# Expert tokens fetched and added back by indirect DMA instead of one-hot matmuls, and expert weights in 4 MB loads over a ring of six units

## The reference, cut to what matters

```python
def expert_choice_moe(xn, w_router, w_gate, w_up, w_down):
    cap = EC_CAPACITY * T // N_EXPERTS            # 2 * 528 // 16 = 66 tokens per expert
    aff = jax.nn.softmax(logits, axis=-1)         # logits = xn @ w_router
    gate, idx = lax.top_k(jnp.swapaxes(aff, 1, 2), cap)
    xe = xn[bidx, idx]                            # 66 rows of 1024 per expert
    hid = jax.nn.silu(xe @ w_gate) * (xe @ w_up)  # w_gate, w_up: 1024 x 2048 per expert
    ye = (hid @ w_down) * gate[..., None]         # w_down: 2048 x 1024 per expert
    return jnp.zeros_like(xn).at[bidx, idx].add(ye)

h = h + expert_choice_moe(rms_norm(h, norm2_g[l]), ...)
return rms_norm(h, final_norm_g)[:, N_META:]
```

## Time and profile before

| | us |
|---|---|
| three timed runs | 2084.88, 2087.76, 2091.49; median 2087.76 |
| profiled execution | 2077.59 |
| its span, first to last instruction | 2075.8 |
| PE busy | 1845.2 (89%) |
| DVE busy | 1356.4 (65%) |
| ACT busy | 1004.0 (48%) |
| POOL busy | 126.2 (6%) |
| queue of SP's and ACT's data (q1), share of 16 engines | 59.5%, 466.12 MB |
| instruction loads (q8) | 187 packets, 3.06 MB |

### The profile page before, as it was taken

One profiled execution on the slowest core, in us unless ns is written; L12 is line 12 of the kernel. 1 busy time (PEld: TensorE's weight loads), 2 busy tenths in 40 slices (PEclk: granted clock), 3 DMA queues, 4 the chain that ended last, 5 costly groups with the idle time before them and its releaser, 6 DMA issues.

```text
span 2075.8 us, 46825 instructions
## 1 busy us (share of the span) xinstructions
PE 1845.2 (89%) x21395; PEld 1346.2 (65%) x21395; DVE 1356.4 (65%) x900; ACT 1004.0 (48%) x627; POOL 126.2 (6%) x101
## 2 busy tenths in 40 slices
PE   4898999889999999946998989898988889899986
PEld 3544863678778888845667666666666667666662
DVE  4422452264343334248899889988988899889994
ACT  4321231142123222134766666676667676667672
POOL 0414043202000000000000000000000000000000
PEclk9798999899999999957999989999999999999997
DMA  9000310123103642005999999999999999999991
GB/s 309 21 21 1 94 34 1 61 62 108 36 21 138 208 151 75 1 26 199 420 380 372 363 378 367 367 363 382 364 357 361 381 374 365 373 380 377 358 362 41
DMA packets 102978, 469.59 MB, mean 226 GB/s; under 512 B 4283, under 2 KB 49659, under 8 KB 86076
## 3 DMA queue, kind: packets, MB, share of 16 engines
q1 hardware_dynamic: 102224, 466.12, 59.5%
q10 hardware_dynamic: 556, 0.32, 0.1%
HBM read 464.32 MB, written 2.10 MB: 225 GB/s over the span
## 4 chain that ended last, share of the span: by engine, by line
PE 64%; DVE 16%; issue 12%; ACT 5%; POOL 2%; DMA 1%; SPq 0%; DVEq 0%; ACTq 0%; POOLq 0%
PE ps_all L1010 22%; DVE wl L941 7%; PE ps_all L1254 6%; PE ps_all L1255 5%; PE ps_all L1256 5%; PE ps_all L1033 5%; PE ps_all L1091 4%; PE ps_all L1242 3%; ACT wh L603 3%; PE ps_all L1240 3%; PE ps_all L1241 3%; PE ps_all L1266 2%; PE ps_all L1222 2%; DVE h L949 2%; DVE tmp L766 1%
## 5 line engine op out<-in xcount | busy, mean ns | idle before, releaser
L941 DVE SCALAR_TENSOR_TENSOR wl<-slot,wh 128x4096 f16<-128x4096 f32 x192 | 847.0, 4419 | 87.4 <-ACT wh L603 87.2
L603 ACT ACTIVATE wh<-slot 128x4096 f16<-128x4096 f32 x192 | 689.3, 3614 | 139.6 <-PE ps_all L1256 90.1
L1240 PE MATMUL ps_all<-xcur,wl 128*128 128x66 f16 x4096 | 402.6, 194 | 46.2 <-DVE wl L941 25.1
L1242 PE MATMUL ps_all<-xcur,wh 128*128 128x66 f16 x4096 | 402.8, 197 | 32.3 <-issue 32.2
L1240 PEld LDWEIGHTS ps_all<-xcur,wl 128*128 128x128 f16 x4096 | 384.7, 100 | 67.8 <-issue 59.4
L1241 PE MATMUL ps_all<-xcur,wh 128*128 128x66 f16 x4096 | 402.4, 194 | 11.3 <-issue 11.3
L1242 PEld LDWEIGHTS ps_all<-xcur,wh 128*128 128x128 f16 x4096 | 383.9, 98 | 37.9 <-issue 37.9
L1241 PEld LDWEIGHTS ps_all<-xcur,wh 128*128 128x128 f16 x4096 | 384.4, 97 | 31.1 <-issue 30.8
L1010 PE MATMUL ps_all<-xnt,wsp 128*128 128x272 f16 (+1 forms) x2688 | 309.6, 278 | 7.0 <-DVE rot L800 5.2
L1010 PEld LDWEIGHTS ps_all<-xnt,wsp 128*128 128x128 f16 x2688 | 265.0, 99 | 52.1 <-issue 8.4
L1254 PE MATMUL ps_all<-wh,hidt 128*66 128x512 f16 x512 | 206.3, 403 | 9.2 <-issue 7.3
(11 more groups left out here) (183 smaller groups left out, 1676.5 us busy)
## 6 DMA issues: line engine op xcount, KB each, us to landing
slot<-in_w_exp_gate SPq DMA_DIRECT2D x64, 2048.0 KB, 9.5
slot<-in_w_exp_up SPq DMA_DIRECT2D x64, 2048.0 KB, 9.8
slot<-in_w_exp_down SPq DMA_DIRECT2D x64, 2048.0 KB, 9.5
raw<-in_w_in SPq DMA_DIRECT2D x32, 1024.0 KB, 5.9
raw<-in_w_ret_out SPq DMA_DIRECT2D x4, 1024.0 KB, 13.6
raw<-in_w_hy_out SPq DMA_DIRECT2D x4, 1024.0 KB, 7.9
raw<-in_w_o SPq DMA_DIRECT2D x4, 1024.0 KB, 5.1
dft_f<-in_c_dft_f SPq DMA_DIRECT2D x1, 2640.0 KB, 20.1
```

Source lines behind the costliest of these rows:

```text
L603: nc.scalar.activation(wh[c % RING][:, :], slot[c % RING][:, :], ACT.Copy, scale=W_S).then_inc(S["w_hi"], 1)
L941: nc.vector.scalar_tensor_tensor(wl[i][:, :], slot[i][:, :], W_S, wh[i][:, :], ALU.mult, ALU.subtract).then_inc(S["w_lo"], 1)
L1240: nc.tensor.matmul(dst, lo, xcur[:, k, 0, :], start=k == 0 and t % TIL == 0, stop=False, skip_group_check=True)
L1242: last = nc.tensor.matmul(dst, hi, xcur[:, k, 1, :], start=False, stop=k == KD - 1, skip_group_check=True)
```

## The change

**Token rows by DMA.** Two DRAM copies are made after the second norm: `h_rows` (the residual) and `xn2_rows` (the normed tokens), both 528 x 1024 float32, stored by POOL. For each expert POOL issues an indirect DMA that fetches 66 rows of `xn2_rows` into `xg` (66 x 1024), named by the column `tok[:, e]` of row numbers, and later one that adds the 66 rows of `ye` to `h_rows` in DRAM. PE turns `xg` with eight float32 transposes in place of the 80 matmuls. `sel`, `st`, `xn2p`, `idxb`, `blki`, `iota`, the scatter and `add_out` go. The gate is applied where ACT takes `ye` out of PSUM. POOL's order is: fetch(0), fetch(1), add(0), fetch(2), add(1), and so on; fetch(e) waits for PE's transposes of expert e - 1, and add(e) for `ye` and for the landing of add(e - 1).

**Weights in 4 MB loads.** A load now brings two units, into one of three slots of 4 MB, so the ring holds six units in place of four. SP waits until both units of the pair three before have their low parts. ACT and DVE still work unit by unit, and `wh`/`wl` remain a ring of four. Three pairs are loaded early (two between the earlier weights, the third after the output projection).

**Ends.** The norm's row `g2b` is loaded before the output projection is done, in place of after it. At the end the four groups of 128 rows are read back from `h_rows` into `hfin`, and the last norm works there.

```diff
+PAIRS = 3
+PAIR_CH = MOE_CH // 2
...
-        def moe_src(e, c):
+        def moe_src(e, j):
+
+            if j < 4:
+
+                m = w_gate if j < 2 else w_up
+                return m[e].rearrange("(p k) n -> p k n", k=KD)[:, 4 * (j % 2):4 * (j % 2) + 4, :]
+
+            return w_down[e].rearrange("(t p) n -> p t n", p=128)[:, 8 * (j - 4):8 * (j - 4) + 8, :]
...
+        def unit(c):
+
+            return pair_slot[c // 2 % PAIRS][:, 4096 * (c % 2):4096 * (c % 2) + 4096]
...
-                if n >= C_A + 1 and n < C_A + 5:
+                if n in (C_A + 1, C_A + 3):
                     if n == C_A + 1:
                         sp.wait_ge(S["yain_split"], KD)
-                    load_first(n - C_A - 1)
+                    load_first((n - C_A - 1) // 2)
...
+            sp.wait_ge(S["tile_done"], AT[("YB", KD - 1)] + 1)
+            sp.dma_start(g2b[:, :], A["norm2_g"][0].partition_broadcast(128)).then_inc(S["g2_row"], 16)
             sp.wait_ge(S["tile_done"], AT[("WO", 3, NT - 1)] + 1)
...
+            load_first(2)
...
             with sp.Fori(1, E) as e:
-                for c in range(MOE_CH):
-                    load(e, c, e * MOE_CH + c - RING + 1)
+                for j in range(PAIR_CH):
+                    load(e, j, e * MOE_CH + 2 * (j - PAIRS + 1))
+            sp.wait_ge(S["rows_landed"], 32 + 16 * E)
+            for k in range(1, NT):
+                sp.dma_start(hfin[:, k - 1, :], h_rows[TS[k][0]:TS[k][0] + 128, :]).then_inc(h_back[k - 1], 16)
...
+            def fetch(e):
+
+                if e:
+                    pool.wait_ge(S["xe_done"], e)
+                pool.indirect_dma_start(xg[:, :], None, xn2_rows[:, :],
+                                        bass.IndirectOffsetOnAxis(ap=tok[:, e:e + 1], axis=0)).then_inc(S["x_in"], 16)
+
+            def add_rows(e):
+
+                pool.wait_ge(S["ye_ready"], e + 1)
+                pool.wait_ge(S["rows_landed"], 32 + 16 * e)
+                pool.indirect_dma_start(h_rows[:, :], bass.IndirectOffsetOnAxis(ap=tok[:, e:e + 1], axis=0),
+                                        ye[:, :], None, compute_op=ALU.add).then_inc(S["rows_landed"], 16)
+
+            for e in range(E):
+                if e + 1 < E:
+                    fetch(e + 1)
+                add_rows(e)
...
             def ye_out(e):
                 act.wait_ge(S["chunk_used"], e * MOE_CH + 12)
+                act.wait_ge(S["rows_landed"], e * 16 + 32)
+                nc.scalar.activation(ye[:, :], ps_all[0:CAP, 3072:4096], ACT.Copy, scale=gate[:, bass.ds(e, 1)]).then_inc(S["ye_ready"], 1)
...
             def gather(e):
 
-                pe.wait_ge(S["sel_ready"], (e + 1) * NT)
+                pe.wait_ge(S["x_in"], 16 * e + 16)
                 for kk in range(KD):
                     c = 512 * (kk // 4) + CAP * (kk % 4)
-                    for k, (_, p) in enumerate(TS):
-                        for q in range(2):
-                            last = nc.tensor.matmul(ps_all[:, c:c + CAP], xn2p[0:p, k, q, kk:kk + KD * 127 + 1:KD], sel[0:p, k, :],
-                                                    start=k == 0 and q == 0, stop=k == NT - 1 and q == 1)
+                    last = nc.tensor.transpose(ps_all[:, c:c + CAP], xg[:, kk:kk + KD * 127 + 1:KD], ident[0:CAP, 0:CAP])
...
-            def scatter(e, k):
...
                 for c in range(MOE_CH):
...
-                    if 2 <= c < 6 and not first:
-                        scatter(e - 1, c - 1)
```

More of the change, by code:

```diff
@@ L137, in job_list @@
     add(("AT",), "work_in", 1)
-    add(("C",), "cols_in", 1)
-    for i in range(2):
-        add(("R", i), "idx_row", i + 1)
+    add(("C",), "cols_in", 2)
     return jobs
@@ L225, in build @@
         ybin = sb("ybin", [128, KD, 2, T], F16, YB)
[L226 to L227 removed]
         xcur = sb("xcur", [128, KD, 2, CAP], F16, XN)
[L229 to L233, removed]
+        hidt = sb("hidt", [128, 2, 16 * CAP], F16, XN + 2112)
+        sg = sb("sg", [128, 16 * CAP], F32, XN + 6336)
+        hid = sb("hid", [128, 16 * CAP], F32, XN + 10560)
+        ye = sb("ye", [CAP, D], F32, XN + 14784)
+        xg = sb("xg", [CAP, D], F32, YA)
+        hfin = sb("hfin", [128, NT - 1, D], F32, YA)
+        gfb = sb("gfb", [128, D], F32, YA + 16384)
         raw = [sb(f"raw{i}", [128, KD, CW], F32, RAW + 8192 * i) for i in range(3)]
         wsp = [sb(f"wsp{i}", [128, 2, KD, CW], F16, SPL + 8192 * i) for i in range(3)]
[L236 to L242, removed]
+        pair_slot = [sb(f"slot{i}", [128, 8192], F32, TOP + 32768 * i) for i in range(PAIRS)]
+        spl_at = [SEARLY, SEARLY + 16384, SLATE, SLATE + 16384]
         wh = [sb(f"wh{i}", [128, 4096], F16, at) for i, at in enumerate(spl_at)]
         wl = [sb(f"wl{i}", [128, 4096], F16, at + 8192) for i, at in enumerate(spl_at)]
[L245 to L247 removed]
+        g2b = sb("g2b", [128, D], F32, SLATE)
+        junk2 = sb("junk2", [128, D], F32, SLATE + 4096)
+        xn2t = sb("xn2t", [128, KD, T], F32, SLATE + 8192)
+        work = sb("work", [E, T], F32, SLATE + 8192 + 16896)
         upad = [sb(f"upad{i}", [128, T + 2], F32, TOP + 2144 * i) for i in range(2)]
@@ L957, in moe @@
                     low(e, c)
-                    if c == 0 and not first:
-                        scatter_map(e - 1)
-                    if c == 3 and not last:
-                        dve.wait_ge(S["xe_done"], e + 1)
-                        select(e + 1)
-                    if 4 <= c < 8 and not first:
-                        add_out(e - 1, c - 3)
                     if c == 8:
@@ L982, in _ @@
             moe(E - 1, False, True)
-            scatter_map(E - 1)
-            for k in range(1, NT):
-                add_out(E - 1, k)
+            dve.wait_ge(S["gf_row"], 16)
             for k in range(1, NT):
@@ L1257, in down @@
                 return last
-            def scatter(e, k):
-                if k == 1:
-                    pe.wait_ge(S["ye_ready"], e + 1)
-                    pe.wait_ge(S["st_ready"], e + 1)
-                else:
-                    pe.wait_ge(S["moe_add"], e * 4 + k - 1)
-                for n in range(2):
-                    last = nc.tensor.matmul(ps_all[:, 3072 + 512 * n:3584 + 512 * n], st[:, 128 * (k - 1):128 * k],
-                                            ye[:, 512 * n:512 * n + 512], start=True, stop=True)
-                last.then_inc(S["scat_done"], 1)
             def moe(e, first, last_one):
@@ L1304, in _ @@
             moe(E - 1, False, True)
-            for k in range(1, NT):
-                scatter(E - 1, k)
 def shape_tables():
```

130 lines of the change are left out of this document (51 added, 79 removed).

## The result

The kernel after took 2121.97 us (median of 4 runs, 2119.31 to 2123.55), the kernel before beside it 2086.32 us: a ratio of 1.0166, 95% interval 1.0143 to 1.0189. I had forecast 2040 and a range up to 2096: wrong in sign and outside the range. Its profiled span is 2120.0 us against 2075.8.

What follows compares the result with a forecast made beforehand. Computation and weight supply were both taken to run at 68.2 us per expert; with supply at 67.0, landing 1991.5, plus 18.4 and 17.4 gave span 2027.4, and with 1.8 and 10.2 added 2040 us, range 1988 to 2096.

Steps and rivals of the forecast that it cites:

- from 9 to 8.2: Loop, supply: PE's instruction packets per expert fall with its matmuls from 960 to 872, priced at 5.0 to 8.0 us.
- rival for the slower side: Loop: indirect additions hold the DMA engines; 70.5 us per expert gives 2094, 72.5 gives 2125; slower or equal 0.21.
- Opening: Before the loop: no wait for `gfb` (-5.0), fetch and transposes for search follow-up and gather (-8), weights' stage +1: -12 us.
- the earlier weights' stage: Opening: 2 MB more of early loads are 4.9 us, partly covered by slack; 1 us added (0 to 5).
- Pace: Loop: 186 units at 67.0 us per expert take 1038.5 us from the first issue at 953, last landing at 1991.5.
- PE behind the last landing: After the last load: high part, two low parts and two `down`, +18.4 us, PE ends at 2010.
- End: After PE's end: `ye` 1.0, indirect addition 4, read back, norm and store; 17.4 us (15 to 26) against 26.8.
- plain supply without instruction packets: Loop: weights 58.9 us plus fetch and addition 1.9 us at 427 GB/s, a floor of 60.8 us per expert.
- ACT waiting tens of us for slots: Sign in the profile after: ACT waits for the slots' loads at tens of us in total, at 375 to 395 GB/s.
- inference that one DMA engine carries all instruction packets: Loop, supply: nine packets per expert share one engine, adding 8.8 us to 58.9, so it needs 67.7 us per expert.
- "computation's pace" rival: Loop: computation sets the pace at 62 to 64.5 us per expert, median 1973 to 2011 us; chance 0.17.
- two sentences from the Trainium skill: Supply: loads fit 2.0 us + bytes/436e3, adding nothing; 358 GB/s per core means at least 70.3 us per expert, trace disagrees.

Runs made afterwards that it cites:

- loop_head: The kernel after with 24 more transposes on PE ahead of the loop, nothing else changed: 1997.1 us, ratio 0.9558 to the kernel before.

## Why the prediction was wrong

The step that failed is the one that has PE's packets per expert fall "from 9 to 8.2" with its matmuls, and the price put on them: time of one DMA engine, for a supply at 67.0 us per expert. They stayed at nine, and the loop took 71.3. I had read the nine instruction packets per expert and asked only what they cost the transfers. What they cost here is PE's time, 13 us of waits for code in a pass, and it depends on where the loop's branch lands: with 48 instructions more ahead of the loop the packets are gone and the pass falls from 72.5 to 63.1 us. Not a term of the sum and not a rival held PE waiting for code, though the trace of before had 4.7 us of such waits in a pass.

My rival for the slower side gives 72.5 us per expert and 2125 us, close to the 72.5 and 2122 that came, but that is luck: it has the additions hold full DMA engines. The weights' queue was at 88.5%, the additions had 33 us, and the kernel with its head moved gained 125 with all of them in place.

Term by term in the span, 2120.0 against my 2027.4:

- *Opening*: the first projection began at 957.0 against 959.5 before, 2.5 sooner where I had 12. From the search's end to it the kernel saved 4.2, not 8: the first fetch took 7.27 to land, not 4 (within its bounds), with 4.28 of POOL's own instruction in it, where the second fetch took 4.2 with 0.97. The search ended 1.7 us later in spite of the 5.0 saved at `gfb`. Its end lies anywhere from 940.4 to 945.3 in the twelve traces with the new opening, and at 938.0 and 943.5 in the two with the old one, so that the earlier weights' stage cost more than my 1 is likely but not shown. The first load of the loop was issued at 961.3, not 953: +8.3.
- *Pace*: from there to the last landing at 2067.2 the 186 units took 71.3 us per expert, not 67.0: +67.4. That is the step above, with the wait for `hidt` and the slower clock in it.
- *PE behind the last landing*: 30.9 us to PE's end at 2098.1, not 18.4: +12.5, since loads were early and PE was late.
- *End*: 21.9, not 17.4: +4.5, of it 1.5 for the addition (5.5, not 4) and the rest in pieces of 1.5 us and less.

The rows of the fetch and of the end, in the kernel after:

```profile
947.09 7.27 DMA xg<-xn_rows,tok
...
2099.53 5.47 DMA h_rows<-ye,tok
2105.00 0.02 issue
2105.01 3.36 DMA hfin<-h_rows
```

What was right: the additions and fetches in the loop are cheap where nothing else is late (1.1 us per expert for the additions; I had 1.9 for both). The plain supply without instruction packets, 58.9 + 1.9 = 60.8, stands 2.3 us under the 63.1 of loop_head, where ACT does wait for loads. One of my signs for the forecast, ACT waiting tens of us for slots, came true in that kernel and not in the one I forecast; its rate, 403 GB/s, is above my 375 to 395. The inference that one DMA engine carries all instruction packets was neither shown nor refuted: the packets and PE's waits vanished together.

The "computation's pace" rival (1973 to 2011) holds the time of the change when its code stays (1997), and its 62 to 64.5 us per expert hold the 63.1. Whether computation sets that pace is not shown: ACT waits both for PE and for loads there, and the DMA share is 1.01. Its chance of 0.17 said nothing of what decides between 1997 and 2122.

The prediction's two sentences from the Trainium skill need a correction each. In "HBM Reference", section Specifications (TRN2), the 358 GB/s are the share of a core whose neighbour streams too, and a core that streams alone is said to measure about 425; the 427 GB/s of the earlier trace rows agree with that, and I had read half of the section. The fit of 2.0 us + bytes/436e3 in "DMA: Bandwidth & Descriptors" stands in its section Anatomy of one DMA and was made for DMAs issued by GpSimd, where the loads here are issued by SP.

The Trainium skill, "Runtime: NRT & Kernel Launch", section Instruction fetch mechanics, gives PE room for 2048 instructions, filled in blocks of 256, and calls crossing a block "mostly hidden". Eight blocks fit what the runs show if one is read ahead: eight touched are read again (nine packets) and nine touched too (ten packets), seven touched stay. That one block is read ahead is my inference from the one packet more than pieces. "Mostly hidden" does not hold here: gaps of about 2.2 us after 127 matmuls of 66 columns, and 4 to 6 right behind the branch. The same section says that a taken branch whose target isn't in the current window of two pages stalls for a load. The gap of 2.42 us at the head agrees with the stall; loop_head doesn't agree with the two pages, since its branch goes back over a loop of seven pieces without a packet.

## What to carry to other kernels

Look for the instruction queue's packets inside a loop, and for "issue" gaps on PE that recur after a fixed number of instructions. If the body is near the number of rows that the engine keeps (here 1776 were kept at one place and not at others), count its rows, waits and register work included, from the head to the end of the 256-row piece in which it stands: here 48 more instructions ahead of the loop were worth 125 us, and 32 cost 16. An edit anywhere ahead of a loop moves its head, so compare two kernels only with both heads in known places, or a change will be judged by its luck: by the place alone, this one was worth anything from a gain of 90 us to a loss of 50.

## What the runs showed of the hardware

- A PE loop of 1776 rows is kept or read again by where it starts: kept with some 250 rows in its first 256-row piece (0 packets), read again with 10, 42 and 202 (9 packets per pass). Where between 202 and 250 the edge lies was not tried; by the count it is 240. A loop of 1957 rows was read again at both places tried, with 9 and 10 packets. It would touch eight pieces at best, so by the count it would never be kept; that was not tried over all places.
- Refills that PE waited for started 7.0 and 6.2 us apart in one pass of the kernel after (1388.79, 1395.82, 1402.06), later ones of the pass down to 3.7 us apart; each was about 1 us long. 32, 16 or 4 KB packets of data beside them made little difference (2122, 2114 and 2129 us).
- Behind an idle stretch of 6.09 us PE was granted 0.50 for some 2.8 us.
- An indirect fetch of 66 rows of 4 KB landed in 4.2 us outside the loop and in 12 in it; the first one took 7.3, with 4.28 us of POOL's instruction in place of 0.97. An addition of the same size took 5.5 at the end and 13 in the loop.
